# Writing the output by tokens: a transpose on TensorE at the end of a two-block network, with each token's scale as a column

## What is computed

```python
def rmsnorm(x, g):
    xf = x.astype(jnp.float32)
    y = xf * lax.rsqrt(jnp.mean(xf * xf, axis=-1, keepdims=True) + EPS)
    return (y * g.astype(jnp.float32)).astype(x.dtype)

def second_block(x, ...):
    for l in range(DEPTH_2):
        ...
        h = rmsnorm(x, g_ffn2[l])
        x = x + 0.5 * swiglu(h, w1_b[l], w3_b[l], w2_b[l])
    return rmsnorm(x, g_final)
```

## Time and profile before

| | us |
|---|---|
| three runs | 2985.99, 2987.75, 2991.82 |
| median | 2987.75 |
| profiled execution | 2988.24 |
| its span | 2986.4 |

### The profile page before, as it was taken

How to read it: one execution, slowest core, us unless ns; L and a number is a source line. 1 busy time by engine, 2 the same in 40 slices (tenths; PEclk the granted TensorE clock), 3 DMA queues, 4 the chain that set the end, 5 groups by cost and what they waited for, 6 DMA issues and landing times.

```text
span 2986.4 us, 41805 instructions
## 1 busy us (share of the span) xinstructions
PE 2835.5 (95%) x16000; PEld 2449.8 (82%) x16000; DVE 2187.5 (73%) x2917; ACT 1498.5 (50%) x1995; POOL 497.3 (17%) x504
## 2 busy tenths in 40 slices
PE   8995999999958999999999999899999999999997
PEld 6674788888847999888888999799998888889996
DVE  6637899999978777666458776887776665687775
ACT  6823788888845444433335444454443332354443
POOL 3214011111012111110113111121111111121111
PEclk9997999999978999999999999999999999999998
DMA  5152999999945555232335646365543332355551
GB/s 215 50 174 90 349 376 373 374 374 380 375 167 140 158 162 157 94 108 88 98 99 135 180 132 177 105 163 148 171 137 99 100 99 94 99 148 156 160 159 57
DMA packets 170155, 516.25 MB, mean 173 GB/s; under 512 B 21600, under 2 KB 22112, under 8 KB 169696
## 3 DMA queue, kind: packets, MB, share of 16 engines
q1 hardware_dynamic: 130176, 422.38, 39.9%
q0 software_dynamic: 37568, 79.72, 12.6%
q10 hardware_dynamic: 2208, 11.43, 1.0%
HBM read 509.24 MB, written 12.58 MB: 175 GB/s over the span
## 4 chain that ended last, share of the span: by engine, by line
PE 81%; DVE 7%; issue 4%; ACT 3%; DMA 2%; POOL 2%; SPq 0%; DVEq 0%; ACTq 0%; POOLq 0%
PE bank L597 27%; PE bank L595 27%; PE bank L596 27%; DVE w_lo L1658 1%; ACT w_hi L1035 1%; PE bank L601 1%; DMA sums<-in_w_b 1%; DVE ft L2033 0%; DMA raw<-in_rec_in 0%; DMA raw<-in_w_b 0%; DVE xT L2084 0%; DMA raw<-in_w_a 0%; POOL mv L1461 0%; DVE st L1748 0%; DVE rsq L2069 0%
## 5 line engine op out<-in xcount | busy, mean ns | idle before, releaser
L1658 DVE TENSOR_TENSOR w_lo<-raw,w_hi 128x1024 fp32r<-128x1024 f32 (+3 forms) x481 | 593.1, 1250 | 286.6 <-ACT w_hi L1035 279.5
L1035 ACT ACTIVATE w_hi<-raw 128x1024 fp32r<-128x1024 f32 (+1 forms) x491 | 507.7, 1046 | 291.1 <-PE bank L597 284.1
L595 PE MATMUL bank<-xf_hi,w_lo 128*128 128x256 f32 x2112 | 593.2, 281 | 48.5 <-DVE xf_lo L2039 22.0
L597 PE MATMUL bank<-xf_hi,w_hi 128*128 128x256 f32 x2112 | 589.8, 279 | 0.0
L596 PE MATMUL bank<-xf_lo,w_hi 128*128 128x256 f32 x2112 | 589.8, 279 | 0.0
L595 PEld LDWEIGHTS bank<-xf_hi,w_lo 128*128 128x128 f32 x2112 | 401.8, 190 | 54.3 <-issue 23.7
L596 PEld LDWEIGHTS bank<-xf_lo,w_hi 128*128 128x128 f32 x2112 | 402.1, 190 | 2.4 <-issue 1.0
L597 PEld LDWEIGHTS bank<-xf_hi,w_hi 128*128 128x128 f32 x2112 | 401.9, 190 | 0.0
L1658 DVE TENSOR_TENSOR w_lo<-raw_more,w_hi 128x1024 fp32r<-128x1024 f32 x249 | 296.6, 1221 | 50.9 <-ACT w_hi L1035 48.2
L597 PE MATMUL bank<-g_hi,w_hi 128*128 128x512 f32 x832 | 327.5, 394 | 0.0
L596 PE MATMUL bank<-g_lo,w_hi 128*128 128x512 f32 x832 | 325.7, 392 | 0.0
(11 more groups left out here) (336 smaller groups left out, 5206.9 us busy)
## 6 DMA issues: line engine op xcount, KB each, us to landing
raw_more<-in_moe SPq DMA_DIRECT2D x249, 512.0 KB, 6.5
raw<-in_moe SPq DMA_DIRECT2D x135, 512.0 KB, 6.6
raw<-in_w_a SPq DMA_DIRECT2D x77, 512.0 KB, 6.4
raw<-in_w_b SPq DMA_DIRECT2D x76, 512.0 KB, 6.1
raw<-in_w_in SPq DMA_DIRECT2D x73, 512.0 KB, 3.6
sums<-in_w_a POOLq DMA_DIRECT2D x88, 256.0 KB, 4.9
sums<-in_w_b POOLq DMA_DIRECT2D x88, 256.0 KB, 4.9
raw<-in_w_a SPq DMA_DIRECT2D x68, 256.0 KB, 6.1
```

What stands on the lines that cost most here:

```text
L595: e.matmul(out, a_lo, b_hi, start=start, stop=False, skip_group_check=partial)
L597: return e.matmul(out, a_hi, b_hi, start=False, stop=stop, skip_group_check=partial)
L1035: e.activation(split_of(k)[0], source_of(k), ACT.Copy).then_inc(s["hi"], 1)
L1658: e.tensor_tensor(lo, source_of(k), hi.bitcast(F32), ALU.subtract).then_inc(s["lo"], 1)
```

## The change

The output now has tokens across the partitions: shape 4 x 128 x 1024 (`TT` = 4 groups of 128 tokens), which the host only reshapes.

- **Gain.** Behind each residual add of the last part VectorE multiplies the tile by its gains into `ft` (`finish`, for `GAINS[p]` being `None`), eight times 128x512.
- **Transposes.** TensorE turns each of the eight tiles of `ft`, 128 tokens at a time: 32 transposes of 128x128 into eight banks. A bank "row g" holds 512 features of one group of tokens; even g holds the tiles of even position, odd g those of odd position.
- **Scale.** The column sums of the squares are made per group of tokens, with `rsq` or `sq` as the weights and one column of ones as the moving operand: eight matmuls with an output of 128x1. `rsq` now lacks the last tile's squares (GpSimd adds six times, not seven), and `sq` brings them. Mean, root and reciprocal work on `rcol`, 128x4.
- **Bank reads.** ScalarE reads the four even banks and VectorE the four odd ones, each multiplied by the token's scale from `rcol`, into `xT`.
- **Table load.** ScalarE computes a root of one column early, behind the square of tile 4, so that the table load of the root happens there.
- **Stores.** SyncE issues four stores of 512 KB, one for each group of tokens, rows of 4 KB for each partition.

```diff
+    for g in range(2 * TT):
+        use(("row", g), "fin_p" if g % 2 else "fin_a", g // 2 + 1, (0, 1, 4, 5, 6, 2, 3, 7)[g])
@@ SyncE
-            for j in range(DT):
-                if j < 2:
-                    e.wait_ge(s["fin_p"], j + 1)
-                else:
-                    e.wait_ge(s["fin_g"], j - 1)
-                e.dma_start(io["out"][:, j, :], xT[:, j, :]).then_inc(s["out"], 16)
-            e.wait_ge(s["out"], 16 * DT)
+            for tt in range(TT):
+                e.wait_ge(s["fin_a"], tt + 1)
+                e.wait_ge(s["fin_p"], tt + 1)
+                e.dma_start(io["out"][tt], xT[:, 2 * tt:2 * tt + 2, :].rearrange("p a n -> p (a n)")).then_inc(s["out"], 16)
+            e.wait_ge(s["out"], 16 * TT)
@@ TensorE
-            statistics(6)
+            rows = {}
+            def to_rows(n, tt):
+                g = 2 * tt + n % 2
+                if g not in rows:
+                    rows[g] = free_bank(("row", g))
+                f = e.transpose(rows[g][:, n // 2 * P:(n // 2 + 1) * P], ft[:, n // 4, n % 4, tt * P:(tt + 1) * P], ident)
+                if n >= DT - 2:
+                    f.then_inc(s["fin"], 1)
+            def tiles_to_rows(first, last):
+                for n in range(first, last):
+                    e.wait_ge(s["fin_g"], n + 1)
+                    for tt in range(TT):
+                        if (n % 2, tt) != (1, TT - 1):
+                            to_rows(n, tt)
+            def sums_of_rows():
+                b = free_bank(("stat", 6))
+                e.wait_ge(s["acc"], 7 * 6 + 6)
+                e.wait_ge(s["sqr"], 8 * 6 + DT)
+                for tt in range(TT):
+                    e.matmul(b[:, tt:tt + 1], rsq[:, tt * P:(tt + 1) * P], ones[:, 0:1], start=True, stop=False)
+                    f = e.matmul(b[:, tt:tt + 1], sq[:, (DT - 1) % 2, tt * P:(tt + 1) * P], ones[:, 0:1], start=False, stop=True)
+                f.then_inc(s["stm"], 1)
+            tiles_to_rows(0, 4)
+            sums_of_rows()
+            tiles_to_rows(4, 6)
+            e.wait_ge(s["fin_g"], DT)
+            for tt in range(TT):
+                to_rows(DT - 2, tt)
+                if tt < TT - 1:
+                    to_rows(DT - 1, tt)
+            for n in range(1, DT, 2):
+                to_rows(n, TT - 1)
@@ ScalarE
+                if p == 6 and n == 4:
+                    e.activation(rcol[:, 0:1], ones[:, 0:1], ACT.Sqrt)
-            for j in range(2):
-                e.activation(xT[:, j, :], xT[:, j, :], ACT.Copy, scale=par("g_final", j)).then_inc(s["fin_a"], 1)
-            root(6)
+            e.wait_ge(s["rs1"], 7)
+            e.activation(rcol[:, :], rcol[:, :], ACT.Sqrt).then_inc(s["rs2"], 1)
+            e.wait_ge(s["rs3"], 7)
+            for tt in range(TT):
+                e.wait_ge(s["fin"], DT + 2 * tt + 1)
+                e.activation(xT[:, 2 * tt, :], bank_of(("row", 2 * tt))[:, :], ACT.Copy, scale=rcol[:, tt:tt + 1]) \
+                    .then_inc(s["fin_a"], 1)
@@ GpSimd
-                squares(p, 5, DT)
+                squares(p, 5, DT if p < 6 else DT - 1)
-            for j in range(2):
-                e.wait_ge(s["fin_a"], j + 1)
-                e.wait_ge(s["rs3"], 7)
-                e.tensor_tensor(xT[:, j, :], xT[:, j, :], rsq[:, :], ALU.mult).then_inc(s["fin_p"], 1)
@@ VectorE
+                if GAINS[p] is None:
+                    e.tensor_scalar(ft[:, n // 4, n % 4, :], xT[:, j, :], par("g_final", j), None, ALU.mult) \
+                        .then_inc(s["fin_g"], 1)
+                    return
-            root(6)
-            for j in range(2, DT):
-                e.scalar_tensor_tensor(xT[:, j, :], xT[:, j, :], par("g_final", j), rsq[:, :],
-                                       ALU.mult, ALU.mult).then_inc(s["fin_g"], 1)
+            e.wait_ge(s["stm"], 7)
+            e.tensor_scalar(rcol[:, :], bank[7][:, 0:TT], 1.0 / D, RMS_EPS, ALU.mult, ALU.add).then_inc(s["rs1"], 1)
+            e.wait_ge(s["rs2"], 7)
+            e.reciprocal(rcol[:, :], rcol[:, :]).then_inc(s["rs3"], 1)
+            e.wait_ge(s["rs3"], 7)
+            for tt in range(TT):
+                e.wait_ge(s["fin"], DT + 2 * tt + 2)
+                e.tensor_scalar(xT[:, 2 * tt + 1, :], bank_of(("row", 2 * tt + 1))[:, :], rcol[:, tt:tt + 1], None,
+                                ALU.mult).then_inc(s["fin_p"], 1)
```

More of the change, by code:

```diff
@@ L391, in build @@
         rsq = sb("rsq", [P, T])
+        rcol = sb("rcol", [P, TT])
         with ExitStack() as ffn:
@@ L2014, in finish @@
             def finish(p, n, name, count):
-                if GAINS[p] is None:
-                    return
                 j = TILES[n]
                 e.wait_ge(s[name], count)
+                if GAINS[p] is None:
+                    e.tensor_scalar(ft[:, n // 4, n % 4, :], xT[:, j, :], par("g_final", j), None, ALU.mult) \
+                        .then_inc(s["fin_g"], 1)
+                    return
                 if not FORMS[p]:
@@ L2494 @@
         args[name] = nc.dram_tensor(f"in_{name}", a.shape, mybir.dt.from_np(a.dtype), kind="ExternalInput").ap()
-    args["out"] = nc.dram_tensor("out_0", (P, DT, T), F32, kind="ExternalOutput").ap()
+    args["out"] = nc.dram_tensor("out_0", (TT, P, D), F32, kind="ExternalOutput").ap()
     build(nc, dram_views(args))
@@ L2498 @@
     got = r.results[0]["out_0"]
-    return got.transpose(2, 1, 0).reshape(1, T, D)
+    return got.reshape(1, T, D)
```

## The result

| | before | after |
|---|---|---|
| median us | 2987.75 (five runs, 2984.98 to 2991.82) | 3017.46 (five runs, 3016.1 to 3020.36) |
| profiled execution | 2988.24 | 3016.1 |
| its span | 2986.4 | 3014.2 |
| last residual add ends | 2967.29 | 3002.15 |
| from there to the end | 19.1 | 12.1 |

The ratio of after to before is 1.0101, with a 95% interval from 1.0086 to 1.0116. So the kernel became about 30 us slower. The part that the prediction worked out, from the last residual add to the end, became 7.0 us shorter (forecast: 6.7). The part that it took as fixed became 34.9 us longer.

What follows compares the result with a forecast made beforehand. With TensorE busy nearly throughout, only the stretch after the last residual add could move, its end set by store bytes. Terms from 2967.29 gave a span of 2979.66, 6.74 us shorter; off the median 2987.75, 2981.0 us (range 2979.3 to 2984.7).

Steps and rivals of the forecast that it cites:

- a residual add of the last swiglu starts later than now: Sign, in the last swiglu before the end, that the forecast is wrong; no size given.
- eleven transposes: TensorE after the last residual add: the transposes left of tiles 0 to 3, 0.11 us each, 1.21 us.
- column sums: TensorE's eight fp32 sums per token group behind eleven transposes, taken as sixteen records of 0.12 us, 1.92 us.
- bank read and issue: VectorE's first bank read with scales, 0.81 us, plus 0.02, then SyncE's issue 0.04 later.
- data: The four output stores of 512 KB, 2.10 MB at 379 GB/s, 5.53 us.
- dear sums: Rival for TensorE's column sums: non-overlapping weight loads, 2982.1 us, or half clock from 2967.33, 2984.3 us; chance 0.17.
- The rival of slow stores: Final stores of whole rows below 171 GB/s end later than before; at 140 GB/s, 2990.5 us; chance 0.04.
- Scale hidden beside transposes: Mean, root and reciprocal after the column sums are ready at 2971.3, hidden beside TensorE's transposes by some 0.3 us.
- Clock: Transposes hold TensorE's full clock at the end; the rival has it fall at 2969.33, 2982.7 us, chance 0.13.
- VectorE's last multiplication by the gain before the last residual add: In the last swiglu it must fit between the adds of tiles 6 and 7, within VectorE's 0.68 us wait.
- their own rule: For the whole time: a quarter of the forecast's 0.62 counts as within 0.2%, a fifth of the 0.17 as faster.
- something else: Remaining case for the whole kernel's time, no size given; chance 0.04.

Runs made afterwards that it cites:

- `rcol` last: The changed kernel with `rcol` placed behind `sq`, at the end of SBUF, so no other tile moves against the kernel before: 2980.06 us, 0.9975 times the kernel before.
- the kernel moved by 192: The changed kernel with unused bytes behind `rcol`, so the second block's tiles begin 192 bytes later than before: 3013.54 us, 1.008 times the kernel before.

## Why the prediction was wrong

**The step that failed** is in the first part: "the change leaves every matmul of the layers where it is, so only what follows the last residual add can move". The matmuls are where they were in TensorE's program, which is what the prediction went by. Their operands are not where they were in SBUF. The diff shows it in one line, `rcol` behind `rsq` and ahead of the whole second block, and it was given no term in the sum. None of the rivals had it, and "a residual add of the last swiglu starts later than now" stood only among what would show the forecast wrong. That row did show it: 3001.46 in place of 2966.60. From the trace of before the size couldn't have been worked out, but a sign was there: the same shape at the same clock, 128x256 with `w` and with `e`, took 279 and 283 ns. What failed is thus this one step: the body was put at nothing and measured 34.9 us. The range had no case in which TensorE's matmuls change, so its upper end was 33 us too low.

**The terms of the end**, each from the last residual add on, were mostly right:

| term | forecast us | after us |
|---|---|---|
| hand-over | 0.04 | 0.06 |
| eleven transposes | 1.21 | 1.26 |
| column sums | 1.92 | 1.70 |
| transposes up to the first read | 1.15 | 1.29 |
| bank read and issue | 0.87 | 0.83 |
| issue to first data | 0.86 | 0.83 |
| data | 5.53 | 5.18 |
| last data to the end | 0.79 | 0.95 |
| sum | 12.37 | 12.10 |

- Column sums: eight instructions of one column, 0.22 us each in the steady part. The sixteen records were right, at 0.11 and not 0.12 each. The weight loads last 0.19 us each and start 0.11 us apart, so they overlap, and both cases of "dear sums" fell.
- Bank reads: 0.68 us (2.73 / 4), not the 0.81 of the earlier trace rows. It stands nearer to the 0.70 of the earlier trace rows, which was kept for the low end. The hand-over to SyncE was 0.15 and took most of that back.
- Stores: 406 GB/s, not 379. The rival of slow stores fell with the sign reversed: four stores of 512 KB in pieces of 4 KB are faster here than eight of 256 KB in pieces of 2 KB.
- Scale hidden beside transposes: right, with 0.5 us to spare against VectorE's read and 0.4 against ScalarE's.
- Clock: right. It stayed at 1.00 from the last swiglu through 32 transposes and the column sums, and fell only after 3009, behind TensorE's last transpose, which ends by 3007.4:

```profile
3008.20:3009.00 0.80, 0.00 (x0) 0.00 (x0) 0.80 (x2) 0.56 (x1) 0.00 (x0) 1.00 1.02 404
3009.00:3010.00 1.00, 0.00 (x0) 0.00 (x0) 0.19 (x1) 0.00 (x0) 0.00 (x0) 0.88 1.00 401
```

  The Trainium skill ("TensorE: Matmul & The Clock Gate", Part 4: PE-mode transpose) says that the full clock does not engage for transposes; the trace disagrees a second time.
- VectorE's last multiplication by the gain before the last residual add: 0.49 us, and VectorE still waits 0.16 us behind it, so it was covered.

The sum came out 0.27 us from the measured end partly by luck: the terms that were too long make 0.64 us, those that were too short 0.37.

With `rcol` last the time was 2980.06 us, and 2981.0 had been forecast. That nearness is in part luck too. Beside its own runs of the kernel before (median 2988.22) it is 8.2 us shorter, not 6.7. The end accounts for 7.0 of them; in the profiled executions the last residual add also ends 1.0 us earlier (2966.25 and 2967.29).

The chances don't follow from their own rule. A quarter of 0.62 and four fifths of 0.17 taken off leave 0.50 for "faster by over 0.2%", at most 0.54 with all of "something else", where 0.55 stands.

**What stays open.** That the spacing follows the distance between the tiles from `xf` on and those ahead of `rcol`, and that 256 bytes more change nothing, is shown, by moving one group against the other and by moving both. That the two that count are the moving operand and the weights is shown nearly as well: moving `e`, with all behind it, against `xf` changed the matmuls with `e`. No run moves `xf` alone, though. Why the distance counts isn't shown. The other engines' work isn't it: among matmuls with VectorE and ScalarE idle the spacing is 113.5 ns in before and 119.7 in after, with GpSimd idle too 113.5 and 119.6, and with no DMA packet under way 114.3 and 119.8. Whether the reads of the moving operand and the weight loads get in each other's way, or something else does, no run separates. The switch between 113.5 and 118 ns at d = 64 is open as well, and so is the slower `g` of the kernel moved by 192.

## What to carry to other kernels

A tile added to a kernel moves every tile allocated behind it, and on a kernel whose TensorE is busy all the time that alone can cost more than the edit brings: put new small tiles behind all others, or compare the places of the matmul operands before and after as part of the change. When a change loses time evenly over stages that it doesn't touch, look at the distance from start to start of the commonest matmul over a long stretch, and try an unused tile of the same size in the old kernel. A forecast of the end of a program from its rows can be good to 0.3 us, here with errors that partly cancel, and still say nothing of the whole.

## What the runs showed that was not expected

- 128x256 matmuls run at 113.5 to 120 ns from start to start at one and the same full clock, and their mean goes by the distance of their operands in SBUF modulo 256 bytes. 128x512 ones (`xg`) run at 227 to 238. On this kernel that is up to 35 us, 1.2%.
- 32 bytes are enough: an unused tile of 16 bytes made the kernel before 1.0116 times as long.
- Stores out of SBUF move at 378 GB/s as eight of 256 KB in pieces of 2 KB, and at 405 GB/s as four of 512 KB in pieces of 4 KB.
- A plain fp32 matmul with one column of output costs 0.22 us at full clock, two transposes' worth (0.11 each).
